# A two-layer diffusion transformer on one core: the state-space scan run in two buffers, thirteen pieces of the conditioning product moved into attention, and the zero fill of a scratch buffer placed later in the load queue

## The reference, cut to what matters

```python
mod_x = split((silu(c) @ w_mod[i] + b_mod[i]), 6)          # and mod_c from c_ctx
u = concat([ada_norm(hc, ..., mod_c[0], mod_c[1]), ada_norm(hx, ..., mod_x[0], mod_x[1])])
proj = u @ w_in[i]
# scan, per chunk of 128 tokens, per direction, per head:
seg = a_cum[:, :, :, None] - a_cum[:, :, None, :]
scores = (C @ B.T) * exp(where(lower, seg, -inf)) * dt
y = scores @ x + C @ h_in * exp(a_cum)
y_ssd = rms_norm((y_f + flip(y_b) + d_skip * x) * silu(z), norm_g)
```

## Time and profile before

| | us |
|---|---|
| median of 3 runs (lowest, highest) | 1500.72 (1498.11, 1502.36) |
| the profiled execution: device time | 1498.55 |
| the profiled execution: span | 1496.4 |
| busy: PE, DVE, ACT, POOL | 1226.1, 465.7, 264.9, 121.3 |
| mean granted TensorE clock | 0.885 of 2.4 GHz |
| DMA moved | 347.83 MB, mean 232 GB/s |

### The profile page before, as it was taken

How to read it: one execution, slowest core, us unless ns; L and a number is a source line. 1 busy time by engine, 2 the same in 40 slices (tenths; PEclk the granted TensorE clock), 3 DMA queues, 4 the chain that set the end, 5 groups by cost and what they waited for, 6 DMA issues and landing times.

```text
span 1496.4 us, 13900 instructions
## 1 busy us (share of the span) xinstructions
PE 1226.1 (82%) x5162; PEld 562.9 (38%) x5162; DVE 465.7 (31%) x1088; ACT 264.9 (18%) x564; POOL 121.3 (8%) x107
## 2 busy tenths in 40 slices
PE   3899887879998379999897299976798399788792
PEld 1363333346653123333232146533466133222231
DVE  2311444656732501111011621465562311001014
ACT  1320101114521311111010322101242111001002
POOL 2000021640000200000000200033100100000001
PEclk9899999995799689999999599986599699899995
DMA  9998109990021399999999310023003599999942
GB/s 348 379 353 310 56 0 383 420 376 2 1 74 39 161 315 378 386 382 378 388 427 339 112 56 1 0 87 137 0 8 161 188 374 387 397 402 389 424 185 91
DMA packets 86029, 347.83 MB, mean 232 GB/s; under 512 B 5958, under 2 KB 37387, under 8 KB 63435
## 3 DMA queue, kind: packets, MB, share of 16 engines
q1 hardware_dynamic: 67056, 308.76, 53.5%
q10 hardware_dynamic: 14907, 24.70, 5.0%
q0 software_dynamic: 4000, 13.49, 2.6%
HBM read 302.89 MB, written 44.04 MB: 232 GB/s over the span
## 4 chain that ended last, share of the span: by engine, by line
PE 64%; DMA 16%; DVE 13%; issue 3%; ACT 2%; POOL 1%; ACTq 1%; SPq 0%; POOLq 0%; DVEq 0%
PE ps L801 17%; PE ps L459 11%; DMA ring<-in_exp_w_up 8%; PE ps L822 7%; PE ps L726 6%; PE ps L468 5%; PE ps L402 4%; DMA ring<-in_w_mod 3%; DMA arena<-in_exp_w_up 3%; PE ps L705 2%; PE ps L424 2%; PE ps L634 1%; PE ps L680 1%; PE ps L622 1%; PE ps L677 1%
## 5 line engine op out<-in xcount | busy, mean ns | idle before, releaser
L801 PE MATMUL ps<-ring,arena 128*64 128x512 f32 x1024 | 235.3, 613 | 26.9 <-DMA ring<-in_exp_w_up 26.9
L402 PE MATMUL ps<-cst,arena 128*128 128x128 f32 x594 | 109.8, 319 | 93.6 <-DMA arena<-slots 37.4
L459 PE MATMUL ps<-u,ring 128*128 128x512 f32 (+1 forms) x416 | 168.8, 566 | 10.0 <-ACT u L1537 6.2
L1422 DVE TENSOR_TENSOR arena<-arena,ps 128x256 f32<-128x256 f32 x44 | 26.8, 610 | 421.1 <-ACT arena L1662 421.1
L402 PEld LDWEIGHTS ps<-cst,arena 128*128 128x128 f32 x594 | 76.1, 162 | 179.7 <-issue 62.3
L801 PEld LDWEIGHTS ps<-ring,arena 128*64 128x64 f32 x1024 | 72.5, 141 | 167.6 <-issue 139.1
L459 PEld LDWEIGHTS ps<-u,ring 128*128 128x128 f32 x416 | 80.2, 195 | 97.3 <-issue 91.1
L822 PE MATMUL ps<-arena 128*64 128x512 f32 x512 | 115.4, 592 | 0.9 <-ACT arena L1666 0.9
L801 PE MATMUL ps<-arena 128*64 128x512 f32 x384 | 91.7, 633 | 15.2 <-DMA arena<-in_exp_w_up 15.2
L726 PE MATMUL ps<-u,ring 128*128 128x512 f32 (+1 forms) x256 | 83.1, 486 | 1.0 <-DVE u L1266 1.0
L468 PE MATMUL ps<-ring,u 128*128 128x256 f32 (+1 forms) x224 | 75.4, 496 | 6.9 <-DVE arena L1129 6.9
(11 more groups left out here) (252 smaller groups left out, 1174.8 us busy)
## 6 DMA issues: line engine op xcount, KB each, us to landing
ring<-in_w_mod SPq DMA_DIRECT2D x24, 2048.0 KB, 14.9
ring<-in_exp_w_gate SPq DMA_DIRECT2D x22, 2048.0 KB, 23.2
ring<-in_exp_w_up SPq DMA_DIRECT2D x22, 2048.0 KB, 28.4
arena<-in_exp_w_down SPq DMA_DIRECT2D x22, 2048.0 KB, 22.2
slots<-zeros SPq DMA_DIRECT2D x4, 6144.0 KB, 41.0
arena<-in_exp_w_gate SPq DMA_DIRECT2D x10, 2048.0 KB, 22.8
arena<-in_exp_w_up SPq DMA_DIRECT2D x10, 2048.0 KB, 28.5
u<-in_exp_w_down SPq DMA_DIRECT2D x10, 2048.0 KB, 25.7
```

The source lines that it names most:

```text
L402: return nc.tensor.transpose(dst, src, ident[0:n, 0:n])
L459: last = nc.tensor.matmul(bank[row:row + width, 0:T - c0], w[:, k, n:n + width], u[:, k, c0:T], start=(k == 0), stop=(k == KT - 1))
L801: last = nc.tensor.matmul(ps[BLOCK * half:BLOCK * half + BLOCK, 2 + b % 2, :].rearrange("p (s n) -> p s n", s=2), x_k, pair[:, :, a:a + 25 ...
L1422: tt(hid.rearrange("p (j c) -> p c j", j=2), silu_g.rearrange("p (c j) -> p c j", j=2), ps[:, 2 + b % 2, 256:512].rearrange("p (c j) -> p ...
```

## The change

Three things are changed.

1. **The scan in two buffers.** `ews`, `gms`, `y_sums` and a fourth `xdt` row are second buffers, laid over `u`, `rt`, `rstd` and `b_tok`, which are free then. PE's list starts with the casts of tile 0 and the first of tile 1. In the loop a tile's y products come first, then the second cast of the next tile, the scores and first cast of the tile after it. DVE, ACT and POOL follow the same order. Waits are added for `xdt_ready`, and for the z products before POOL writes into `u`.
2. **Thirteen modulation parts moved.** `SCAN_MODS` leaves 7 parts in layer 0's scan; the last 13 run in steps 2 to 14 of layer 0's attention, one after each step's scores. Since bank 7 is the modulation's then, all 256-key units transpose into bank 6 (`turned_probs`), and a transposition waits for the copy of the unit just before it instead of the one before that.
3. **The zero fill** is issued after the last `w_out` chunk of layer 0 instead of ahead of z.

```diff
+SCAN_MODS = (1, 1, 1)
+MODS_LEFT = 13
...
+        ews = [[ew[:, d] for d in range(2)],
+               [u[:, k:k + 2, :].rearrange("p k t -> p (k t)").rearrange("p (h i) -> p h i", i=P) for k in (0, 6)]]
+        gms = [gm, rt[:, 0:8, :, :].rearrange("p s t e -> p (s t e)").rearrange("p (d g i) -> p d g i", d=2, i=P)]
+        y_sums = [y_acc, rstd[:, :]]
...
@@ PE, scan_tiles @@
+                scores(0)
+                for d in range(2):
+                    cast_rows(0, d)
+                    spare(SCAN_MODS[0])
+                scores(1)
+                cast_rows(1, 0)
+                for i, t in enumerate(tiles):
                     if i == 0:
                         pe.wait_ge(S("states_done"), l + 1)
                     else:
                         pe.wait_ge(S("y_banks_read", l), i)
                     for d in range(2):
+                        pe.wait_ge(S("xdt_ready"), 2 * tiles_before(l) + 2 * i + d + 1)
                         pe.wait_ge(S("w_ready", l), 2 * i + d + 1)
...
                     last.then_inc(S("y_summed", l), 1)
-                    if i > 0:
+                    if i + 1 < len(tiles):
+                        cast_rows(i + 1, 1)
+                        spare(SCAN_MODS[1])
+                    if i + 2 < len(tiles):
+                        scores(i + 2)
+                        cast_rows(i + 2, 0)
+                        spare(SCAN_MODS[2])
+                    if i:
                         y_transposes(l, t - 1, i)
-                    spare(1)
@@ PE, attention @@
+                    spare(mod_in_attention(l, s))
...
-                        if n >= 2:
+                        if n >= 1 and units[n - 1][3] == NCTX:
+                            pe.wait_ge(S("probs_t_ready"), before + n)
+                            if nk > NCTX:
+                                pe.wait_ge(S("mod_placed"), DEPTH * DEPTH_GROUPS)
+                        elif n >= 2:
                             pe.wait_ge(S("probs_t_ready"), before + n - 1)
@@ DVE, scan_tiles @@
+                masked_scores(0)
+                for d in range(2):
+                    clamp(0, d)
+                    spare(SCAN_MODS[0])
+                masked_scores(1)
+                clamp(1, 0)
+                for i, t in enumerate(tiles):
                     if i:
+                        y_norm(l, t - 1)
+                    if i + 1 < len(tiles):
+                        clamp(i + 1, 1)
                     dve.wait_ge(S("y_summed", l), i + 1)
...
+                    if i + 1 < len(tiles):
+                        spare(SCAN_MODS[1])
+                    if i + 2 < len(tiles):
+                        masked_scores(i + 2)
+                        clamp(i + 2, 0)
+                        spare(SCAN_MODS[2])
+                    if i:
+                        y_turned(l, t - 1)
@@ ACT, scan @@
+                decays(0, 0)
+                decays(0, 1)
+                decays(1, 0)
+                for i in range(n):
+                    if i + 1 < n:
+                        decays(i + 1, 1)
                     act.wait_ge(S("y_gated", l), i + 1)
...
+                    if i + 2 < n:
+                        decays(i + 2, 0)
@@ POOL @@
+                pool.wait_ge(filled, max(entry[f"z{l}{t}"] for t in tiles) + 1)
+                rows(1, 0)
+                rows(1, 1)
+                weights(0, 0)
+                weights(0, 1)
+                x_dt(1, 0)
+                weights(1, 0)
+                for i in range(len(tiles) - 1):
+
+                    pool.wait_ge(S("y_summed", l), i + 1)
+                    x_dt(i + 1, 1)
+                    if i + 2 < len(tiles):
+                        rows(i + 2, 0)
+                        rows(i + 2, 1)
+                    weights(i + 1, 1)
+                    if i + 2 < len(tiles):
+                        x_dt(i + 2, 0)
+
+                    pool.wait_ge(S("y_gated", l), i + 1)
+                    skip(i + 1)
+                    if i + 2 < len(tiles):
+                        weights(i + 2, 0)
@@ SP @@
-                if key == ("in", 0, "z", 0):
-                    sp.wait_ge(S("zeros_ready"), 1)
...
+            sp.wait_ge(S("zeros_ready"), 1)
             experts(0)
```

More of the change, by code:

```diff
@@ L606, in scan_tiles, with scores @@
             def scan_tiles(l):
-                first = FIRST_T[l]
-                for i, t in enumerate(range(first, TT)):
+                tiles = range(FIRST_T[l], TT)
+                def scores(i):
+                    t = tiles[i]
                     for g in range(2):
@@ L650, in y_transposes @@
                 for m in range(4):
-                    last = tr(bank[:, P * m:P * m + P], y_acc[:, P * m:P * m + P])
+                    last = tr(bank[:, P * m:P * m + P], y_sums[(t - FIRST_T[l]) % 2][:, P * m:P * m + P])
                 close_bank(last)
@@ new lines, in scan_tiles, with masked_scores, clamp @@
+                tiles = range(FIRST_T[l], TT)
+                def masked_scores(i):
+                    if i >= 2:
+                        dve.wait_ge(S("w_ready", l), 2 * (i - 1))
+                    for g in range(2):
+                        bank = claim(f"cb{l}{tiles[i]}{g}")
+                        for d in range(2):
+                            last = tt(gms[i % 2][:, d, g, :], bank[:, 0:P], tri[d], ALU.mult)
+                        emptied(last)
+                def clamp(i, d):
+                    dve.wait_ge(S("rows_cast", l), 2 * i + d + 1)
+                    for hh in range(SSD_H):
+                        last = ts(ews[i % 2][d][:, hh, :], ps[:, 2 + hh // 4, P * (hh % 4):P * (hh % 4) + P],
+                                  sc[:, 8, 32 * d + 8 * tiles[i] + hh:32 * d + 8 * tiles[i] + hh + 1], 0.0,
+                                  ALU.subtract, ALU.min)
+                    last.then_inc(S("decay_clamped", l), 1)
@@ new lines, in skip, with weights @@
+                def skip(i):
+                    g.tensor_tensor(y_skip.rearrange("p (m a n) -> p m a n", m=4, a=2), xs(tiles[i]),
+                                    xb(bcast[:, l, B_D:B_D + 8]), ALU.mult).then_inc(S("skip_ready"), 1)
+                def weights(i, d):
+                    pool.wait_ge(evacuated, entry[f"cb{l}{tiles[i]}1"] + 1)
+                    pool.wait_ge(S("decay_exp", l), 2 * i + d + 1)
+                    for gg in range(2):
+                        part = ews[i % 2][d][:, 4 * gg:4 * gg + 4, :]
+                        last = g.tensor_tensor(part, part, gms[i % 2][:, d, gg, :].unsqueeze(1).to_broadcast(
+                            [P, 4, P]), ALU.mult)
+                    last.then_inc(S("w_ready", l), 1)
@@ new lines, in _ @@
+                rows(0, 0)
+                rows(0, 1)
+                pool.wait_ge(filled, entry[f"state{l}{len(state_steps(l)) - 1}"] + 1)
+                x_dt(0, 0)
+                x_dt(0, 1)
+                skip(0)
+                pool.wait_ge(filled, max(entry[f"z{l}{t}"] for t in tiles) + 1)
[18 more added lines that the diff above has]
+                        weights(i + 2, 0)
@@ L1904, in _ @@
                         load_tokens(2 * ring_at[key] + t)
+            sp.wait_ge(S("zeros_ready"), 1)
+            for k in range(ZERO_DMAS):
+                n = ROWS * DM // (P * ZERO_DMAS * 256)
+                sp.dma_start(slots.rearrange("(z p r) n -> z p (r n)", z=ZERO_DMAS, p=P)[k].rearrange(
+                    "p (r n) -> p r n", n=256), zeros[:, :].unsqueeze(1).to_broadcast([P, n, 256])).then_inc(
+                    S("zeros_stored"), 16)
             experts(0)
```

131 lines of the change are left out of this document (50 added, 81 removed).

## The result

| | before | after |
|---|---|---|
| median, us (lowest, highest, runs) | 1501.07 (1498.11, 1502.36, 4) | 1477.30 (1476.48, 1478.24, 4) |
| profiled execution: device time, span, us | 1498.55, 1496.4 | 1477.52, 1475.7 |
| mean granted clock, of 2.4 GHz | 0.885 | 0.894 |

The ratio is 0.9845, 95% interval 0.9826 to 0.9864: faster by 23.8 us. The forecast was 1474 us, in a range of 1464 to 1494, with 0.90 on faster.

The account below looks back on a forecast made before the run. Layer 0's scan was taken as bound by full DMA and work going round all engines, attention by PE at half clock. 1498.55 - 31 + 7 - 2.5 gave 1472 us profiled, 1474 median, range 1464 to 1494.

Parts of the forecast that it names:

- What bounds the scan: Layer 0's scan: DMA full throughout, no engine full, because a tile's work goes round them all.
- The zeros at 0: Moving the zero fill behind `w_out`: gains nothing and costs 0, hidden by attention and the output projection.
- Layer 0's scan, -29: Layer 0's scan with two buffers and fewer parts: 59 us, 29 less than before.
- two rivals: Layer 0's scan: clock falls there (12 in 100); POOL and DVE hold each other up (12 in 100).
- the term's bound of -21: Layer 0's scan with its tail, taken at -31: -21 if each add and each POOL instruction held the other up.
- the POOL rival: Layer 0's scan: POOL and DVE hold each other up, 17.5 us a tile, 1484 us; 12 in 100.
- The tail, -2: Behind layer 0's last y product: DVE's adds begin at once instead of after placing the tile before, 2 us less.
- Attention, +7: Layer 0's attention with 13 parts: clock rises, steps 2 to 15 take 43 us; +7, from +4 to +38.
- Layer 1's scan, -2.5: Layer 1's scan, two tiles without parts: gate earlier, taken at -2.5 us, from 0 to -6.
- The added waits cost nothing: Waits before POOL's rows in `u` and for `xdt_ready`: no cost, since POOL is idle before the first weights.
- Sum: Whole kernel's profiled execution: 1498.55 - 31 + 7 - 2.5 = 1472 us; median 1474.
- The signs of being wrong: L622 lasting 3.7 us in layer 0, attention's parts 3.6, or POOL's rows delaying casts over 3 us a tile.

Follow-up runs that it names:

- e2: Changed kernel with all 20 modulation parts in layer 0's scan (dealt 1, 4, 3), none in attention: 1501.44 us, ratio 0.9998 to the kernel before.
- e10: Changed kernel with all 20 parts in layer 0's scan, dealt 2, 4, 2, none in attention: 1504.03 us, ratio 1.0008 to the kernel before.
- e3: Kernel before with only the 13 parts moved into attention, scan still in one buffer: 1506.89 us, ratio 1.0034 to the kernel before.
- e1: Changed kernel with the zero fill back ahead of z's chunk, nothing else: 1476.2 us, ratio 0.9821 to the kernel before.
- e9: Changed kernel with the products of attention's parts cut to 50 of 160 records, loads, waits and transposes kept: 1479.81 us in one execution.
- e12: Changed kernel with POOL's tile 1 rows behind rotate's ropes, DVE's adds ahead of the clamp, and attention's parts in steps 0 to 12: 1462.21 us, ratio 0.976.
- e4: Changed kernel with POOL's rows of tile 1 waiting until DVE has finished the rotation: 1474.84 us, ratio 0.981 to the kernel before.
- e7: Changed kernel with a loop turn's last part ahead of the first cast (clamp) of the tile after next: 1485.38 us, ratio 0.9897 to the kernel before.

## Why the prediction was right, point by point

**What bounds the scan** was read rightly and used incompletely. The argument named both the full DMA and the round through the engines, and costed the two edits together. It never asked what either is worth alone; e2, e10 and e3 give 0, 0 and -0.3% of gain.

**The zeros at 0** held. They were issued from 348.8 us (forecast: 340) for 60 us, and e1 finds no price. The first expert product stood at 519 us where 509 was written; the sum's own terms give 510 (534.3 - 31 + 7).

**Layer 0's scan, -29.** Measured -25.2; the y distances are 13.2, 18.0 and 15.1 us where 13.0, 14.9 and 12.1 were written. Tile 1 is right. Tile 2 is 3.1 us over: POOL's rows lasted 4.20 us beside DVE's adds, not 3.75, PE waited 3.15 us for them, and the cast behind ran at half clock. Tile 3 is 3.0 over: 2.46 us until the banks are free, as the lists said, and then products at 3.67 in place of 2.00 us, which they did not say. So a small piece of two rivals came true: the clock fell twice, and POOL and DVE held each other up a little. Both lay inside the term's bound of -21. (For the third distance the POOL rival's 17.5 us a tile would give +5.4, not the 3 that it has.)

**The tail, -2.** Last y product to the scores of step 2 took 9.2 us, before 11.1: -1.9.

**Attention, +7.** Step 2 to output projection went from 87.9 to 97.8 us: +9.9. The clock rose as forecast: the part at 314.04 took 3.50 us, the next ones 1.92. The shortfall has two places. Steps 2 to 15 took 46.0 us, not 43; 3.3 of it are waits for chunks, taken at 1, and 1.6 the part at half clock behind the second. And the four steps after them took 13.1 us, not 11.5, since the clock fell once more behind the 1.55 us wait for the single bank. e9 and e12 show that the term rests on too little: PE's work was summed (41.9 of the 46.0 us), but when the last parts run is set by their chunks. The sum came near because the two are about equally long, which was luck. On the Trainium skill's rule (TensorE: Matmul & The Clock Gate, "The HAM clock gate"), by which activity of the engine releases the throttle, the runs speak on both sides: the rise at 317 us behind one part agrees with it, the full PE of the earlier trace rows at 0.50 does not.

**Layer 1's scan, -2.5.** Measured -8.4, outside the bound of -6, and +2.6 in the stretch ahead of it. The sum took PE's durations at 1.5, 1.0 and 1.9 times, and no rise. In the profile the clock rose for one tile, and that makes 7.7 of the 8.4 us; in e1, where it did not, the term is -0.7. So the term's size was not found by its argument in either case.

**"The added waits cost nothing".** This is the step that failed. It asked whether POOL is early enough with its rows in `u`, and it is. It did not ask what runs on DVE meanwhile: rotate's ropes with two inputs in SBUF, two of which last 2.0 us and more in place of 0.42 beside POOL's 3.9 us. The price was 3.2 us in layer 1 and 0.7 in layer 0, shown by e4. The argument had the means: it priced the same effect between adds and POOL, in the scan only. The Trainium skill (SBUF — State Buffer, "SBUF: two separate sides") has the two engines share a port pair under an exclusive lock for the length of an instruction, for a DVE instruction with two inputs in SBUF too; the two instructions end 0.2 and 0.3 us behind POOL's two halves of 1.96 us, so the trace agrees in the main (one that ran only behind POOL's would end 0.4 us behind it).

**Sum.** Forecast -26.5 us for the profiled execution, measured -21.0: the scan with its tail 3.9 worse, attention 2.9, rotate about 4, the start of the run about 1, layer 1's scan 5.9 better, and some tenths elsewhere. That the time came within 3.3 us of the forecast is in part luck: half of what went wrong was given back by a clock in layer 1 that the argument did not foresee. The range would have held without it. The terms' own bounds, added up, give 1466 to 1487 us (attention at +4 to +7), not the 1464 to 1484 that stand in the text.

**The signs of being wrong** were touched, once or twice each, and not met throughout: one cast in layer 0 lasted 3.57 us, two parts in attention 3.50 and 3.51, and POOL's rows held one cast back by 3.15 us. What they were to tell apart (half clock in every tile, in every part, POOL as the path of each tile) did not come.

## What to carry to other kernels

When a stretch has two limits of nearly the same length (here a DMA stream of 84 us and a round through the engines of 81), cost each half of the change alone too: neither may show anything without the other. And when a term comes out much better than its argument, look for the clock in its rows before crediting the change: 7.7 us of layer 1's 8.4 were that. A filler piece of work is not free to stand anywhere in an engine's list; look for whom it waits and how far behind that producer stands in its own list (a wait of 3.15 us became 8.29 in e7), and for a stream through a ring ask first when the first slot comes free, since that took 3.0 us off attention and cutting two thirds of the parts' work took off nothing. Work that is put early "because its engine is idle" must be held against what the other engine does at that time.

## What the runs showed of the hardware that was not expected

- With 50 records of 128x512 products left of 160, the granted clock was 0.92 in 320 to 330 us and 1.00 in 330 to 345. Before the change PE was busy for all of 350 to 371.6 us with products of at most 256 columns at 0.50. In 330 to 345 us PE was busy for 10.31 of 15 us. Which property of those few products makes the difference stays open.
- Half clock came behind short waits: 3.15 us (the cast then 3.57 in place of 1.98), 2.46 (products 3.67 in place of 2.00), 1.94 (a part 3.51 in place of 1.92). The kernel before had passed waits of up to 3.1 us at full clock, so the length of the one wait doesn't decide.
- The same instructions behind the same wait of 1.61 us, in layer 1's scan, ran at full clock in one execution and at half in another: 34.6 against 42.3 us for the scan, in kernels that there are alike.
- Two rope instructions of 0.42 us took 2.09 and 2.00 us beside one POOL instruction pair of 3.93.
